# Block one attention: fill products in another order, memory keys and values as pairs in one bank

## The reference, cut to what matters

```python
for l in range(DEPTH):
    h = _rmsnorm(x, g_pre_mix[l])
    z = h @ w_in[l]
    zf, zq, zk, zv, zm = jnp.split(z, splits, axis=-1)      # 256, 512, 128, 128, 256 channels
    y_f = _fourier_mix(zf, w_fourier[l])                    # real part of fftn over tokens and channels, then w_f
    q = _rope(zq.reshape(b, s, N_Q_HEADS, HEAD_DIM), positions)
    k = _rope(zk.reshape(b, s, N_KV_HEADS, HEAD_DIM), positions)
    v = zv.reshape(b, s, N_KV_HEADS, HEAD_DIM)
    y_a = _window_attn(q, k, v, sink[l])                    # keys up to 128 tokens away, softmax with a sink
    mkv = _rmsnorm(mem, g_mem[l]) @ w_mem_kv[l]
    km, vm = jnp.split(mkv, 2, axis=-1)
    y_m = _memory_attn(zm.reshape(b, s, N_MEM_HEADS, HEAD_DIM), km, vm)
    y = jnp.concatenate([_rmsnorm(y_f, ...), _rmsnorm(y_a, ...), _rmsnorm(y_m, ...)], axis=-1) @ w_out[l]
    x = x + _rmsnorm(y, g_post_mix[l])
    ...
```

## Time and profile before

| | us |
|---|---|
| median of three runs | 3403.66 |
| lowest and highest run | 3401.55, 3404.52 |
| the profiled execution | 3403.3 |
| its span, first to last instruction | 3401.1 |

### The profile page before, as it was taken

The page is one execution under the profiler, slowest core; times in us unless marked ns, Lnnn a source line. Parts: engine busy times, 40 slices in busy tenths (PEclk is TensorE's granted clock), DMA queues, the critical chain, the costliest instruction groups (busy, mean ns, idle before and its releaser), DMA issues. The chain is left out here.

```text
span 3401.1 us, 49530 instructions
## 1 busy us (share of the span) xinstructions
PE 3346.8 (98%) x19557; PEld 2878.0 (85%) x19557; DVE 2446.4 (72%) x3484; ACT 1631.7 (48%) x2405; POOL 77.0 (2%) x98
## 2 busy tenths in 40 slices
PE   7999999999999999999999999999999999999999
PEld 5679988778998899887678899889988768889997
DVE  8669854759872888468885698459864888659863
ACT  4645643455652556226523365426642562335642
POOL 1010000100000000000000000000000000000000
PEclk9999999999999999999999999999999999999999
DMA  4123323213332233332232333333333223233332
GB/s 144 50 75 112 112 90 109 88 57 88 112 112 99 87 112 113 102 102 63 65 96 90 99 112 100 102 108 101 112 106 99 77 63 87 87 99 111 102 104 87
DMA packets 341658, 326.29 MB, mean 96 GB/s; under 512 B 31992, under 2 KB 312388, under 8 KB 341444
## 3 DMA queue, kind: packets, MB, share of 16 engines
q1 hardware_dynamic: 335588, 307.95, 28.6%
q0 software_dynamic: 4064, 13.50, 1.8%
q10 hardware_dynamic: 1792, 1.88, 0.2%
HBM read 313.84 MB, written 2.10 MB: 93 GB/s over the span
## 5 line engine op out<-in xcount | busy, mean ns | idle before, releaser
L2233 DVE TENSOR_TENSOR w_lo<-raw,w_hi 128x2048 fp32r<-128x2048 f32 x190 | 435.2, 2290 | 478.1 <-ACT w_hi L1559 477.3
L1559 ACT ACTIVATE w_hi<-raw 128x2048 fp32r<-128x2048 f32 x190 | 363.7, 1914 | 820.9 <-PE products L818 543.7
L962 PE MATMUL products<-seven_x,w_hi 128*128 128x256 f32 x2592 | 464.3, 279 | 0.0
L818 PE MATMUL products<-a_hi,w_hi 128*128 128x512 f32 (+1 forms) x1056 | 425.3, 403 | 4.5 <-DVE X L3319 2.7
L818 PE MATMUL products<-a_hi,w_lo 128*128 128x512 f32 (+1 forms) x1056 | 411.8, 390 | 0.0
L818 PE MATMUL products<-a_lo,w_hi 128*128 128x512 f32 (+1 forms) x1056 | 411.4, 390 | 0.0
L962 PEld LDWEIGHTS products<-seven_x,w_hi 128*128 128x128 f32 x2592 | 395.0, 188 | 0.5
L962 PE MATMUL products<-seven_x,more_hi 128*128 128x256 f32 x1632 | 375.8, 279 | 0.0
L962 PE MATMUL products<-seven_x,w_lo 128*128 128x256 f32 x1296 | 361.2, 279 | 0.0
L962 PEld LDWEIGHTS products<-seven_x,more_hi 128*128 128x128 f32 x1632 | 277.6, 188 | 0.0
L818 PEld LDWEIGHTS products<-a_hi,w_hi 128*128 128x128 f32 (+1 forms) x1056 | 197.9, 187 | 54.4 <-issue 11.5
(11 more groups left out here) (473 smaller groups left out, 7440.5 us busy)
## 6 DMA issues: line engine op xcount, KB each, us to landing
raw<-in_ffn_w SPq DMA_DIRECT2D x244, 512.0 KB, 4.2
raw<-in_w_in SPq DMA_DIRECT2D x108, 512.0 KB, 4.6
raw<-in_w_ffn_in SPq DMA_DIRECT2D x88, 512.0 KB, 4.2
raw<-in_w_ffn_out SPq DMA_DIRECT2D x40, 512.0 KB, 4.4
raw<-in_w_out SPq DMA_DIRECT2D x32, 512.0 KB, 4.2
raw<-in_ffn_w SPq DMA_DIRECT2D x24, 384.0 KB, 3.3
x_sums<-x_sums POOLq DMA_DIRECT2D x12, 512.0 KB, 6.2
raw<-in_w_mem_kv SPq DMA_DIRECT2D x8, 512.0 KB, 3.9
```

The costliest lines, as they stand in the source:

```text
L818: mm = pe.matmul(G[pair][0:m, into + b, 0:n], w[:, s, at:at + m], x, start=(first or into > 0) and k == 0 and q == 0, stop=(last or ends) ...
L962: mm = pe.matmul(out, ww[:, cut], xx[:, part], start=starts and k == 0 and q == 0, stop=name in ("P2", "P3", "P4") and k == 3 and q == 2, ...
L1559: act.activation(w_hi[:, s, :], raw[:, s, :], ACT.Copy).then_inc(hi_ready, 1)
L2233: dve.tensor_tensor(w_lo[:, s, :], raw[:, s, :], w_hi[:, s, :].bitcast(F32), ALU.subtract).then_inc(lo_ready, 1)
```

## The change

The fills get another order. Steps 0 to 2 compute zm (step 0 both halves of the first tile, steps 1 and 2 one half each of the second). Step 3 computes both memory-key tiles side by side in the one bank, step 4 both memory-value tiles; DVE evicts each pair with one instruction. Step 5 transposes the values and computes the first half of zf's first tile, step 6 its second half, step 7 both halves of zf's second tile. Steps 8 and 9 have two Fourier tiles each, step 10 all Fourier rows. The splits of the next weights stand at the end of steps 2, 3 and 5 instead of 2, 4 and 5, SP loads zf's weights after the memory keys' and values', the folds get a semaphore of their own, and the DFT table waits for six fills.

```diff
@@ sync: order of the weight units
                 tall("w_in", l, 4 * P)
-                tall("w_in", l, 0)
                 tall("w_in", l, 8 * P)
                 for j in range(2):
                     tall("w_mem_kv", l, 2 * P * j)
+                tall("w_in", l, 0)
                 by_tokens("w_out", l, MIX_UNITS)
@@ tensor
-                def fill_tile(hi, lo, b, part, parts=2, n=SEQ):
-
-                    if part == 0:
-                        if b == 0:
-                            take_unit()
-                        if c.fills:
-                            pe.wait_ge(fill_read, c.next("fill_read"))
-                        c.fills += 1
+                def fresh_fill(unit=False):
+
+                    if unit:
+                        take_unit()
+                    if c.fills:
+                        pe.wait_ge(fill_read, c.next("fill_read"))
+                    c.fills += 1
...
+                def memory_fill(b):
+
+                    s = (c.unit - 1) % 2
+                    for k in range(DC):
+                        for q, (w, x) in enumerate(((w_hi, m_hi), (w_hi, m_lo), (w_lo, m_hi))):
+                            mm = pe.matmul(fill_bank[:, b * MEM:(b + 1) * MEM], w[:, s, (k * 2 + b) * P:(k * 2 + b + 1) * P],
+                                           x[:, k, :], start=k == 0 and q == 0, stop=k == DC - 1 and q == 2)
+                    if b:
                         mm.then_inc(fill_done, 1)
...
+                    if i == 0:
+                        if part == 0:
+                            fresh_fill(unit=True)
+                        half_fill(0, part)
+                    elif i in (1, 2) and part == 0:
+                        if i == 1:
+                            fresh_fill()
+                        half_fill(1, i - 1)
+                    elif i in (3, 4):
+                        if part == 0:
+                            fresh_fill(unit=True)
+                            if i == 3:
+                                pe.wait_ge(al_ready, c.next("al_ready", DC))
+                        memory_fill(part)
+                    elif i == 5 and part == 0:
+                        pe.wait_ge(fill_read, c.now("fill_read") + 1)
                         for j in range(4):
                             mm = pe.transpose(fill_bank[:, j * P:(j + 1) * P],
                                               vmT[:, j % 2, (j // 2) * P:(j // 2 + 1) * P], ident[:])
                         mm.then_inc(swap_ready, 1)
-                    elif i == 6:
+                    elif i == 5:
+                        fresh_fill(unit=True)
                         pe.wait_ge(swap_copied, c.next("swap_copied"))
-                        pe.wait_ge(four_copied, c.next("four_copied"))
-                        fourier_tile(0)
+                        half_fill(0, 0)
+                    elif i == 6 and part == 0:
+                        half_fill(0, 1)
                     elif i == 7:
-                        fourier_tile(1 + part)
-                    elif i == 8 and part == 0:
-                        fourier_tile(3)
-                    elif i in (9, 10):
-                        fourier_rows(i - 9, part)
+                        if part == 0:
+                            fresh_fill()
+                        half_fill(1, part)
+                    elif i == 8:
+                        if part == 0:
+                            pe.wait_ge(fill_read, c.next("fill_read"))
+                            pe.wait_ge(folded_ready, c.next("folded_ready", 2))
+                            pe.wait_ge(four_copied, c.next("four_copied"))
+                        fourier_tile(part)
+                    elif i == 9:
+                        fourier_tile(2 + part)
+                    elif i == 10:
+                        for columns in range(2):
+                            fourier_rows(part, columns)
@@ scalar: copies and splits in step i
-                    if i in (7, 8):
+                    if i in (8, 9, 10):
                         fourier_copy()
...
-                    if i in (2, 4, 5, 10):
-                        act.wait_ge(fill_done, c.next("fill_done", 2))
+                    if i in (2, 3, 5, 10):
+                        act.wait_ge(fill_done, c.next("fill_done", 2 if i in (2, 10) else 1))
                         split_hi()
@@ vector: evictions and splits in step i
+                    if n in (2, 3):
+                        dve.tensor_tensor((kmT, vmT)[n - 2][:], fill_bank.rearrange("p (b n) -> p b n", b=2),
+                                          wide(rs_b[:, 0:MEM], 2), ALU.mult).then_inc(fill_read, c.one("fill_read"))
+                        return
...
-                        for n_fill in {1: (0,), 2: (1,), 3: (2,), 4: (3,), 5: (5,), 6: (7,)}.get(i, ()):
-                            fill_evict(n_fill)
+                        if i in (1, 3, 4, 5, 7, 8):
+                            fill_evict((1, 3, 4, 5, 7, 8).index(i))
                         if i >= 2:
                             out_evict(i - 2)
...
-                    for n_fill in {4: (4,), 5: (6,)}.get(i, ()):
-                        fill_evict(n_fill)
...
-                    if i in (2, 4, 5):
+                    if i in (2, 3, 5):
                         split_lo()
@@ gpsimd
-                pool.wait_ge(fill_done, c.next("fill_done", 4))
+                pool.wait_ge(fill_done, c.next("fill_done", 6))
```

More of the change, by code:

```diff
@@ L534, in two_blocks @@
         t_ready, pt_ready, o_ready, o_used = (sem(n) for n in ("t_ready", "pt_ready", "o_ready", "o_used"))
-        fill_done, fill_read = sem("fill_done"), sem("fill_read")
+        fill_done, fill_read, folded_ready = sem("fill_done"), sem("fill_read"), sem("folded_ready")
         gate_zeroed, gate_loaded = sem("gate_zeroed"), sem("gate_loaded")
@@ L1220, in _, with half_fill @@
                 c.group += 1
-                def fill_tile(hi, lo, b, part, parts=2, n=SEQ):
-                    if part == 0:
-                        if b == 0:
-                            take_unit()
-                        if c.fills:
-                            pe.wait_ge(fill_read, c.next("fill_read"))
-                        c.fills += 1
+                def fresh_fill(unit=False):
[4 more added lines that the diff above has]
+                    c.fills += 1
+                def half_fill(b, part):
                     s = (c.unit - 1) % 2
-                    for k in range(part * DC // parts, (part + 1) * DC // parts):
-                        for q, (w, x) in enumerate(((w_hi, hi), (w_hi, lo), (w_lo, hi))):
-                            mm = pe.matmul(fill_bank[:, 0:n], w[:, s, (k * 2 + b) * P:(k * 2 + b + 1) * P], x[:, k, :],
+                    for k in range(part * DC // 2, (part + 1) * DC // 2):
+                        for q, (w, x) in enumerate(((w_hi, a_hi), (w_hi, a_lo), (w_lo, a_hi))):
+                            mm = pe.matmul(fill_bank, w[:, s, (k * 2 + b) * P:(k * 2 + b + 1) * P], x[:, k, :],
                                            start=k == 0 and q == 0, stop=k == DC - 1 and q == 2)
-                    if part == parts - 1:
+                    if part:
+                        mm.then_inc(fill_done, 1)
+                def memory_fill(b):
[5 more added lines that the diff above has]
+                    if b:
                         mm.then_inc(fill_done, 1)
@@ L1976, in _ @@
                         turn_copy(n_turned + 1)
-                    if i == 6:
+                    if i == 5:
                         act.wait_ge(swap_ready, c.next("swap_ready"))
                         act.activation(vm_tok[:], fill_bank, ACT.Copy).then_inc(swap_copied, 1)
-                    if i in (7, 8):
+                    if i in (8, 9, 10):
                         fourier_copy()
@@ L1987, in _ @@
                         n_turned += quads[i - 1]["n"] // P
+                    if i in (8, 9, 10):
+                        fourier_copy()
                     if i == 9:
@@ L1991, in _ @@
                             act.activation(mix_squares[chunk], y_mix[:, chunk, :], ACT.Square).then_inc(sq_ready, 1)
-                    if i in (6, 7, 9, 10):
-                        fourier_copy()
                     if i == 11:
@@ L2914, in fill_evict @@
                     dve.wait_ge(fill_done, c.next("fill_done"))
[L2915 to L2918, removed]
+                    if n in (2, 3):
+                        dve.tensor_tensor((kmT, vmT)[n - 2][:], fill_bank.rearrange("p (b n) -> p b n", b=2),
+                                          wide(rs_b[:, 0:MEM], 2), ALU.mult).then_inc(fill_read, c.one("fill_read"))
+                        return
+                    b = n % 2
+                    dve.tensor_tensor((zmT if n < 2 else zfT)[:, b, :], fill_bank, rs[:], ALU.mult).then_inc(
                         fill_read, c.one("fill_read"))
-                    if n < 2:
+                    if n >= 4:
                         dve.wait_ge(fill_read, c.now("fill_read"))
```

(10 more changed lines are left out.)

## The result

The changed kernel takes 3417.42 us (median of six runs, 3414.95 to 3420.29), the kernel before 3402.81 beside it (six runs, 3401.55 to 3406.99): the ratio is 1.0042, with a 95% interval of 1.0032 to 1.0053. The change makes the kernel slower. Forecast were 3413.3 us and a range of 3407.5 to 3418.

A forecast was written before the change was run, and what follows sets the result against it. TensorE (PE) was taken as the bound, busy 3346.8 of 3401.1 us. New waits of 8.6 less old 3.6 make 5.0 us a layer: 3403.3 + 2 x 5.0 = 3413.3 us, 8-in-10 range 3407.5 to 3418.

The forecast's parts named there:

- step 6: PE waits before the third product for ACT's copy, after DVE's split and the softmax work: 2.1 us a layer.
- turn 1: In step 2, with a half tile less to cover the softmax chain, PE waits for scaling 1: 1.0 us a layer.
- third product of step 2: PE waits there for the copy of the third turn: 0.5 us a layer.
- step 3: PE's memory keys wait for the eviction of zm's second tile, queued behind the weights' low parts: 2.1 us a layer.
- step 4: PE's memory values wait for the memory keys' eviction, queued on DVE behind the moved third split: 1.9 us a layer.
- values' copy: In step 5 Fourier's first half tile waits for the transposed values to be copied off the bank: 0.3 us a layer.
- Fourier copies: Each second Fourier tile in a step waits for ACT's copy of the one before: three places, 0.7 us together.
- The old waits: PE's waits in steps 6 to 9 of the kernel before, 3.6 us a layer: all the change can win here.
- the clock: Rival, 0.06: three waits of 2 us a layer each drop PE's clock to half; 3431 us, or 3422 if it recovers.
- two prices per fall: Up to 3 us if the next 3.05 of a fill runs at half speed, half that if it recovers within the fill.
- The faster rival: Evictions come free before PE wants the bank, because DVE reaches them before the splits' high parts are ready: 3396.1 us, chance 0.07.
- The first half of the loop ends where it ended: Despite 6.8 us less PE work, the loop's first half gains nothing: softmax chain and splits eat all of it.

The follow-up runs named there:

- queries_early: Changed kernel with only the eviction of the queries (zm's second tile, step 3) moved ahead of its split, to the end of step 2: 3411.82 us, ratio 1.0019.
- keys_early: Changed kernel with only the eviction of the memory keys (step 4) moved ahead of its split, to the end of step 3: 3412.22 us, ratio 1.0021.
- split_at_4: Changed kernel with the third split of weights put back to the end of step 4 on ACT and DVE, evictions left: 3410.29 us, ratio 1.0018.
- old_split_at_3: Kernel before with only the third split issued at the end of step 3 instead of step 4: 3410.42 against 3404.21 us, ratio 1.0017.
- both_early: Changed kernel with the evictions of zm's second tile and the memory keys moved ahead of the splits of steps 2 and 3: 3405.32 us, ratio 1.0001.
- beside_exp: both_early with the low parts of step 5's split moved behind the maxima of quad 6, beside ACT's exponentials: 3401.88 against 3404.21 us, ratio 0.9992.
- old_beside_exp: Kernel before with only the low parts of step 5's split moved behind the maxima of quad 6: 3404.01 against 3404.21 us, ratio 1.0000.

## Why the prediction was right, and where it was off

**The side and the cause were right.** The three waits it named for evictions and for step 6 stand where it put them and end by DVE and ACT as it said, and the loop grew, not shrank. From turn 6 on it grew by 5.08 us (30.88 before, 35.96 after), where the prediction had 5.2; up to turn 6 it had no change, and the measured 1.49 (63.52 to 65.01) is the slow clock of step 4. Its terms, from start to start: turn 1 1.0, measured 1.07; third product of step 2 0.5, measured 0.37; step 3 2.1, measured 2.28; step 4 1.9, measured 2.16; values' copy 0.3, measured 0.37; step 6 2.1, measured 1.87; Fourier copies 0.7, measured 0.58. Together 8.6 against 8.7: the count through the queues of PE, ACT and DVE holds to 0.3 us in every term. The old waits, 3.6, went as said; no bracket of 0.5 or more is left in steps 7 to 9 but the score's.

**The mis-sized term is the clock.** Of the 4.1 us between 3413.3 and 3417.42 3.0 are the slow clock behind step 4's wait, 1.5 in each layer; in the profiled execution a fall in the second block adds 1.6, and baselines and scatter take the difference. The prediction held the clock as a rival with 0.06. The lower of its two prices per fall was right (the fill at half speed for a part, 1.5; the upper was 3), its number was not: one fall in each layer, not three, and none was in the forecast. The step that failed is the choice of the nearest row: a stretch with PE at work for 1.72 of 3.30 us at 1.00 was taken as the sign that 2 us of standing do no harm. The runs show that the same wait is harmless in one layer and not in the other (queries_early, keys_early), so one row of one execution can't exclude it. That the 4.1 us stayed inside the range is due to two falls in place of the six that the rival priced; nothing in the prediction told how many there would be, and that part is luck. The Trainium skill (TensorE: Matmul & The Clock Gate, "A second HAM failure mode: psum-queue depth-cycling") says that short idle times of TensorE between groups of matmuls, where they are frequent enough, send the clock back and forth. The traces agree only in part: the clock fell behind single waits of 1.65 to 2.04 us.

**What it put down to the wrong part.** It says of step 4 that "before, the two halves were evicted apart", beside the split. split_at_4 and old_split_at_3 part the two: with the pair and without the early split there is no wait, with the early split and without the pair there is one of 1.92. The split's place alone decides.

**The faster rival** named the right hinge: DVE has to reach the evictions of steps 3 and 4 before the split. both_early made it so and got 3405.32, not 3396.1, because that rival also took away the waits of the softmax chain, of step 6 and of the copies, which both_early still has: 1.07 + 0.37 + 0.37 + 1.87 + 0.58 = 4.3 a layer, against 3.6 won. **"The first half of the loop ends where it ended"**: its reason was chain and splits; it was the splits nearly alone. With them out of the way (beside_exp) the loop up to turn 6 takes 57.5 us (132.61 - 75.08), 6.0 less than before, of the 6.8 of work that left it, and the whole loop is 0.9 shorter, since steps 6 to 9 are covered now.

## What to carry to other kernels

In an in-order queue, put the instruction that frees a bank ahead of any instruction that waits for another engine. Look hardest at a split or copy that waits for the same fill to end: here 0.68 us of eviction behind 2.2 us of split cost 2.2 us a place, and one such move alone (old_split_at_3) cost more in a layer than the 0.9 us that the new order won in its best version. When a reorder empties a step, write down the chain that was hidden in it (here 6.9 us of softmax), and take work to the step where the chain is longest against PE's own work.

## What the runs showed of the hardware that was not expected

TensorE's clock fell to 0.50 behind single waits of 1.65 to 2.04 us, and never in the loops of the traces whose longest bracket was 1.13 or less (before, old_beside_exp, beside_exp and its second run). Such a wait is no sure sign: the loops of the other seven traces hold 29 brackets of 1.65 to 2.04 us, and behind 14 of them the clock fell. It is not a function of the wait alone: in queries_early the bracket of 1.92 was followed by 0.57 in layer one (112 to 116) and by 1.00 in layer two (665 to 669). A fall cost 1.5 us behind steps 3 and 4, where a dense fill follows, and about 1.0 behind step 6 (both_early's loops, 96.05 with and 95.06 without), where PE waits 0.51 for DVE before the next score in layer two and, with the fall, has no bracket there in layer one.

One more fall came between 2720 and 2740, in the second block, in the profiled executions of the changed kernel and of queries_early and in none of the others. No wait of PE stands close before it. In both traces PE does the work of the following row first (here of the changed kernel), sixteen matmuls of one column each, which take 1.78 us up to the next matmul; the matmuls become longer 0.3 us after that (1.5 us in queries_early):

```profile
2733.09 1.92 PE L904 MATMUL small<-ones,craw_sq 128*128 128x1 f32 x16
```

PE counts as busy all that time. The same row stands in the nine other traces without a fall behind it, so what brings a fall there, as behind the waits, is open.
